# The last stage of a decoder step: residual rows read before the stage, and their sum moved from VectorE to Pool

## The chip, the cores and the metric

The kernel runs on one core of a Trainium2 chip. The metric is the device time of one execution in microseconds (us), the median of several. The engines are TensorE (PE, its weight loads PEld), VectorE (DVE), ScalarE (ACT), GpSimd (POOL, called Pool here) and SyncE (SP), which here only issues transfers. Each engine runs its own instructions in order; semaphores tie them together.

## The reference

One layer of a decoder step over 2048 prompt tokens and 32 sample tokens, 1024 channels. Two mixers and a mixture of experts (top 2 of 32) each add to the residual stream, and a last RMS norm follows. The part that matters here is the end:

```python
x = x + gate1 * (merged @ w_o)                 # x_after_mixers, kept in DRAM
...
y = routed_experts(h2, idx, wts, ...)          # two weighted rows for each token, summed
x = x + gate2 * y
...
y_prompt = x * rsqrt(mean(x * x) + EPS) * normf_g     # the same for y_sample
```

## The kernel before

The program has three blocks: `condition`, `sweep_mixers` and `finish`. The last part of `finish` is `experts`. Its main loop runs over blocks of 128 gathered rows, one expert to a block; each block ends with a scatter (L1913, an indirect transfer from Pool) of the weighted rows to `weighted_rows` in DRAM, two rows for each token. A transfer to `expert_gate_up` or `expert_down` brings an expert's weights into a ring of four slots.

After the last block comes the **last stage**, with which the change is concerned. It runs over 17 tiles: 16 of 128 tokens, and tile 16 with the 32 sample tokens. The work on tile i goes through all engines:

- SP reads the tile's pairs (`pairs`, L1792, 1 MB: two rows for each token) into one of NB = 4 buffers `pair`. Three lie in `expert_down`, the fourth in `gathered`.
- TensorE adds the two rows of each pair with 8 matmuls by the identity (L2204) into two banks of PSUM (named `fin` in the profile), and raises `paired`.
- VectorE multiplies by the gate row (L2109, two halves of 512 columns), raises `weighted`, adds the sum to the residual rows `xc(i)` (L2114), and raises `summed`.
- ScalarE squares the row and sums the squares (L2042, `sumsq`). Pool turns the sum into 1/rms with two small operations (L1941 `mean`, L1943 `root`), in the function `rms`. VectorE multiplies the row by it and by the norm's gain (L2118, the function `norm`, `done`), and ScalarE issues the store (L2047).

VectorE's order is `add(i)`, `norm(i - 1)`, so that the round over ScalarE and Pool for tile i - 1 has the time of `add(i)`. A pair buffer is free once `summed` is raised: then SP reads the pairs of tile i + 4.

The residual rows lie in the ring of the gate and up weights, which is free by then: `late_rows` gives NX = 8 places, in slots 0 and 2, and puts the three gate and gain rows into slot 1. Rows 0 to 7 are read before the stage, as soon as the slots are free (L1871). Rows 8 to 16 are read within the stage (L1895): the row of tile i + 8 takes the place of tile i, so SP waits until tile i's output is stored (`out_stored`). SP's own order puts this wait between the reads of pairs.

Of the kernel before, what the change touches and what calls it, by code (L numbers as in the profile page):

```python
# [7 lines left out]
F32 = mybir.dt.float32  # L8
# [3 lines left out]
ALU = mybir.AluOpType  # L12
# [129 lines left out]
def wait_apart(eng, sem, value, passed):  # L142

    eng.wait_ge(sem, value)
    eng.sem_inc(passed, 1)
# [1602 lines left out]
    return lists, ends_i, rest, on_vector, on_tensor  # L1748


def late_rows(ring):

    slot = lambda n: ring[:, n * GU:(n + 1) * GU].rearrange("p (k d) -> p k d", d=D)
    gates = [slot(1)[:, k, :] for k in range(3)]
    return (lambda at, m: slot(2 * (at % 8 // 4))[0:m, at % 4, :]), gates


def experts(nc, a, s, kept, sb, sem, ps, ring, downs, listing, ready, outs):
# [19 lines left out]
    down, y_out, stored = sem("e_down"), sem("e_y_out"), (sem("e_stored0"), sem("e_stored1"))  # L1778
    rec_in = [sem(f"e_rec_in{n}") for n in range(5)]
    x1_in, gates_in = sem("e_x1_in"), sem("e_gates_in")  # L1780
    NB, NX = 4, 8
    g_in, out_stored, late_in = [sem(f"c_pairs_in{k}") for k in range(NB)], [sem(f"c_stored{k}") for k in range(NX)], [sem(f"c_x1_in{k}") for k in range(NX)]
    paired, weighted, summed = sem("c_paired"), sem("c_weighted"), sem("c_summed")
    sumsq, mean, root, done = sem("c_sumsq"), sem("c_mean"), sem("c_root"), sem("c_done")
    xc, (gate, gate_s, gf) = late_rows(ring)
    sq = ring[:, GU + 3 * D:GU + 4 * D]
    pair = [downs[:, n * DOWN:(n + 1) * DOWN].rearrange("p (k d) -> p k d", k=2) for n in range(3)] + [xg[:, :, :]]
    t, minus_half = ready["rms"], kept["half"]
# [26 lines left out]
    def on_sync(sp):  # L1815
# [47 lines left out]
        for slot in (2, 3):  # L1863
            down_arrived(slot, NE // RING)

        x1, gates = late_rows(ring)
        for n, e in ((0, NE - 4), (1, NE - 2)):
            wait_apart(sp, w_lo, last_block(e) * 2, passed)
            for k in range(4):
# [2 lines left out]
            if n == 0:  # L1872
# [3 lines left out]
                             .to_broadcast([DEC_B, DEC_T, D])).then_inc(gates_in, 16)  # L1876
                sp.dma_start(gates[2], a["normf_g"].unsqueeze(0).to_broadcast([P, D])).then_inc(gates_in, 16)
        rest, total = listed(sp, REST, 0), listed(sp, TOTAL, 0)
        wait_apart(sp, stored[0], rest * 16 + 16, passed)
        wait_apart(sp, stored[1], total // 2 * 16, passed)  # L1880
        for n in range(3):
# [5 lines left out]
        for i in range(NT):  # L1887
            sp.wait_ge(summed, i + 1)
            if i + NB <= NT:
                pairs(sp, i + NB, P if i + NB < NT else MS)  # L1890
            late = i + NX - 2
            if i >= 2 and late <= NT:
                m = P if late < NT else MS
                sp.wait_ge(out_stored[(i - 2) % NX], 16 * ((i - 2) // NX + 1))
                sp.dma_start(x1(late, m), s["x1"][late * P:late * P + m, :]).then_inc(late_in[late % NX], 16)  # L1895

    def on_gpsimd(pool):
        pool.wait_ge(ready["lists"], 1)
        pool.wait_ge(ready["stored_x1"], 16 * (NT + 1))
        pool.wait_ge(ready["stored_h2"], 16 * (NT + 1))  # L1900

        def gather(b, slot, landed, first=False):

            if not first:
                wait_apart(pool, x_turned, b - 1, passed)
            wait_apart(pool, idx_in[slot], landed, passed)
            pool.indirect_dma_start(out=xg[:, slot % 2, :], out_offset=None, in_=s["h2"],  # L1907
                                    in_offset=bass.IndirectOffsetOnAxis(ap=idx[:, slot, 0:1].bitcast(U32), axis=0),
                                    bounds_check=TOKENS - 1, oob_is_err=False).then_inc(x_in[slot % 2], 16)

        def scatter(b, slot):
            wait_apart(pool, y_out, b + 1, passed)
            pool.indirect_dma_start(out=s["y2"], out_offset=bass.IndirectOffsetOnAxis(ap=rec[:, slot, 0:1].bitcast(U32), axis=0),  # L1913
                                    in_=y[:, half(slot), :], in_offset=None,
                                    bounds_check=2 * TOKENS - 1, oob_is_err=False).then_inc(stored[half(slot)], 16)

        def step(b, slot, landed):
            gather(b + 2, (slot + 2) % 4, landed)
            scatter(b - 1, (slot - 1) % 4)

        gather(0, 0, 16, True)
        gather(1, 1, 16, True)
        gather(2, 2, 16)
        total = listed(pool, TOTAL, 0)
        step(1, 1, 16)
        step(2, 2, 32)
        step(3, 3, 32)
        with pool.Fori(1, QUADS) as q:
            with pool.If(q * 4 < total):
                step(q * 4, 0, q * 16 + 16)  # L1930
                step(q * 4 + 1, 1, q * 16 + 16)
            with pool.If(q * 4 + 2 < total):
                step(q * 4 + 2, 2, q * 16 + 32)
                step(q * 4 + 3, 3, q * 16 + 32)
        rest = listed(pool, REST, 0)
        scatter(rest * 2 + 1, LAST)

        def rms(i, m):
            k = i % NB
            pool.wait_ge(sumsq, i + 1)  # L1940
            pool.tensor_scalar(t[0:m, k, 1:2], t[0:m, k, 0:1], 1.0 / D, EPS, ALU.mult, ALU.add).then_inc(mean, 1)  # L1941
            pool.wait_ge(mean, i + 1)
            pool.tensor_tensor(t[0:m, k, 2:3], t[0:m, k, 1:2], minus_half[0:m, :], ALU.pow).then_inc(root, 1)  # L1943

        for i, m in tiles():
            rms(i, m)
        wait_apart(pool, stored[0], rest * 16 + 16, passed)
        wait_apart(pool, stored[1], rest * 16 + 16, passed)

    def on_scalar(act):  # L1950
# [93 lines left out]
        def store(i, m):  # L2044
            dst = outs[0][0, i * P:(i + 1) * P, :] if i < NT else outs[1].rearrange("b t d -> (b t) d")
            act.wait_ge(done, i + 1)
            act.dma_start(dst, xc(i, m)).then_inc(out_stored[i % NX], 16)  # L2047

        for i, m in tiles():
            square(i, m)  # L2050
            if i:
                store(i - 1, P)
        store(NT, MS)
        for k in range(NX):
            act.wait_ge(out_stored[k], 16 * (NT // NX + (1 if k == 0 else 0)))
        for slot in range(4):
            wait_apart(act, idx_in[slot], (rest * 2 + (10 - slot)) // 4 * 16, passed)
            wait_apart(act, rec_in[slot], (rest * 2 + (6 - slot)) // 4 * 16, passed)
# [1 line left out]
    def on_vector(dve):  # L2060
# [40 lines left out]
                step(p * 2, 0)  # L2101
                step(p * 2 + 1, 1)

        def add(i, m):
            k, rows = i % NB, gate if i < NT else gate_s
            dve.wait_ge(paired, i + 1)
            for h in range(2):
                at = slice(h * 512, (h + 1) * 512)
                last = nc.vector.tensor_tensor(pair[k][0:m, 0, at], ps[2 * k + h][0:m, :], rows[0:m, at], ALU.mult)  # L2109
            last.then_inc(weighted, 1)  # L2110
            if i >= NX:
                dve.wait_ge(late_in[i % NX], i // NX * 16)
            dve.wait_ge(weighted, i + 1)
            nc.vector.tensor_tensor(xc(i, m), xc(i, m), pair[k][0:m, 0, :], ALU.add).then_inc(summed, 1)  # L2114

        def norm(i, m):
            dve.wait_ge(root, i + 1)
# [1 line left out]
                                           op0=ALU.mult, op1=ALU.mult).then_inc(done, 1)  # L2119

        dve.wait_ge(gates_in, 48)
        dve.wait_ge(x1_in, 16 * NX)
        for i, m in tiles():
            add(i, m)
            if i:
                norm(i - 1, P)
        norm(NT, MS)
# [86 lines left out]
def finish(nc, a, s, kept, outs):  # L2214

    with ExitStack() as ctx:
# [15 lines left out]
        with ExitStack() as gates:  # L2232
# [9 lines left out]
            g = gate_a(nc, a, s, kept, sem, ps, weights, shared)  # L2242
            b = gate_b(nc, a, s, kept, sem, ps, weights, shared, small, ready, early)
        late["ring"] = sb("expert_gate_up", [P, RING * GU])
        ready["split_weights"] = [[sb(f"gate_up{n}_{part}", [P, GU], F32R) for part in ("hi", "lo")] for n in range(2)]
        downs = sb("expert_down", [P, RING * DOWN])
        e = experts(nc, a, s, kept, sb, sem, ps, late["ring"], downs, listing, ready, outs)
# [57 lines left out]
```

## Time and profile before

| | us |
|---|---|
| median of 3 runs | 2117.55 |
| lowest and highest of the runs | 2117.15, 2119.03 |
| the profiled execution's own time | 2116.99 |
| its span, first to last instruction | 2114.6 |
| TensorE busy | 1954.3 |
| VectorE busy | 1090.1 |
| ScalarE busy | 752.9 |
| Pool busy | 329.8 |

The time of an execution is its span and what lies around it (2.4 us here). All places in the program are given in us from the start of the span. The last stage is the stretch from about 2020 us to the end. TensorE's busy share is that of the whole program, in which the stage is 1 part in 22; what bounds the stage has to be read from its own rows.

### The profile page before, as it was taken

The numbers are of one execution on the slowest core, as the hardware profiler recorded it, in microseconds if no ns is written. First come the engines' busy times: TensorE is split into PE (matmuls) and PEld (weight loads), VectorE is DVE, ScalarE is ACT, GpSimd is POOL, SyncE is SP. The second block draws the span as 40 slices with busy tenths as digits, with TensorE's granted clock in tenths as the row PEclk, the third lists the DMA queues.
The fourth block names the chain that finished last, engine by engine and source line by source line (L and its number), as shares of the span: only waits on it lengthen the run. The fifth ranks groups of instructions, "written<-read, shape, count | busy, mean of one in ns | idle before, by whom it ended". The sixth has DMA issues, their size and how long they took to land.

```text
span 2114.6 us, 29676 instructions
## 1 busy us (share of the span) xinstructions
PE 1954.3 (92%) x9239; PEld 1467.3 (69%) x9240; DVE 1090.1 (52%) x1905; ACT 752.9 (36%) x1318; POOL 329.8 (16%) x337
## 2 busy tenths in 40 slices
PE   6599999999869999999899999994699999999876
PEld 2487878778547777776788888873576777677532
DVE  2377777777440000003455555555566666666656
ACT  2245545444230101012321111111466666666611
POOL 0011100111000000000101111111143334333311
PEclk9799999999779999999999999996799999999988
DMA  9322222222185545544744444427487545889577
GB/s 297 105 92 92 102 102 100 102 84 94 30 290 198 193 160 189 206 159 165 270 143 149 146 145 149 143 70 261 150 301 272 213 163 176 296 284 363 202 286 282
DMA packets 193060, 381.87 MB, mean 181 GB/s; under 512 B 43113, under 2 KB 122137, under 8 KB 186828
## 3 DMA queue, kind: packets, MB, share of 16 engines
q1 hardware_dynamic: 153262, 313.07, 41.7%
q0 software_dynamic: 22000, 59.66, 7.4%
q10 hardware_dynamic: 17760, 8.67, 1.4%
q8 instruction: 20, 0.33, 0.1%
q14 instruction: 18, 0.15, 0.0%
HBM read 296.47 MB, written 104.26 MB: 189 GB/s over the span
## 4 chain that ended last, share of the span: by engine, by line
PE 62%; DMA 5%; DVE 2%; SPq 1%; issue 1%; ACT 0%; ACTq 0%; POOL 0%; DVEq 0%; POOLq 0%
PE fin L253 16%; PE fin L255 15%; PE fin L254 15%; PE fin L2169 8%; PE fin L2138 2%; PE fin L1605 1%; DMA expert_down<-weighted_rows 1%; PE fin L1632 1%; DMA w_gate_raw<-in_w_in 1%; DMA mixer_parts<-oT_split 1%; PE fin L2204 1%; PE fin L1184 1%; DMA slot_records<-slot_record,route_slots 1%; DMA pb_b<-out_b_projected 1%; PE fin L2157 0%
## 5 line engine op out<-in xcount | busy, mean ns | idle before, releaser
L2073 DVE TENSOR_TENSOR gate_up_lo<-expert_gate_up,gate_up_hi 128x2048 fp32r<-128x2048 f32 x102 | 233.6, 2292 | 147.4 <-ACT gate_up_hi L1977 143.4
L1977 ACT CAST gate_up_hi<-expert_gate_up 128x2048 fp32r x102 | 194.3, 1906 | 90.4 <-issue 90.4
L253 PE MATMUL mix<-w_mix_hi,hT_hi 128*128 128x512 f32 (+3 forms) x544 | 203.5, 374 | 3.9 <-DVE hT_lo L632 2.6
L254 PE MATMUL mix<-w_mix_hi,hT_lo 128*128 128x512 f32 (+3 forms) x544 | 198.9, 366 | 0.0
L255 PE MATMUL mix<-w_mix_lo,hT_hi 128*128 128x512 f32 (+3 forms) x544 | 198.5, 365 | 0.0
L1127 DVE SCALAR_TENSOR_TENSOR ma_rows<-tanh_rows,fin 128x512 f32<-128x512 f32 (+1 forms) x34 | 21.8, 683 | 339.1 <-PE fin L255 188.6
L2169 PE MATMUL fin<-expert_down,hidden_T 128*128 x400 | 183.0, 601 | 5.5 <-ACT hidden_T L1985 5.5
L253 PE MATMUL fin<-gate_up_hi,gathered_T_hi 128*128 128x512 f32 x400 | 162.0, 405 | 4.2 <-DVE gathered_T_lo L2064 4.2
L255 PE MATMUL fin<-gate_up_lo,gathered_T_hi 128*128 128x512 f32 x400 | 158.1, 395 | 0.0
L254 PE MATMUL fin<-gate_up_hi,gathered_T_lo 128*128 128x512 f32 x400 | 157.6, 394 | 0.0
L1907 POOL DMA_INDIRECT gathered<-h_rows,row_tokens x52 | 130.9, 2517 | 42.4 <-issue 23.9
L2169 PEld LDWEIGHTS fin<-expert_down,hidden_T 128*128 128x128 f32 x400 | 73.2, 193 | 79.4 <-issue 79.3
L253 PEld LDWEIGHTS mix<-w_mix_hi,hT_hi 128*128 128x128 f32 (+1 forms) x544 | 100.6, 185 | 37.2 <-issue 20.3
L253 PE MATMUL fin<-w_gate_hi,h_parts 128*128 128x512 f32 (+1 forms) x272 | 110.8, 407 | 14.2 <-DMA h_parts<-hT_split 12.1
L255 PEld LDWEIGHTS mix<-w_mix_lo,hT_hi 128*128 128x128 f32 (+1 forms) x544 | 100.5, 185 | 19.2
L254 PEld LDWEIGHTS mix<-w_mix_hi,hT_lo 128*128 128x128 f32 (+1 forms) x544 | 100.8, 185 | 16.4
L1913 POOL DMA_INDIRECT weighted_rows<-y_block,row_records x50 | 62.5, 1250 | 305.8 <-ACT y_block L1993 293.9
L253 PE MATMUL fin<-w_out_hi,merged_T_hi 128*128 128x512 f32 (+1 forms) x272 | 107.8, 396 | 1.1 <-ACT merged_T_hi L1387 1.1
L254 PE MATMUL fin<-w_gate_hi,h_parts 128*128 128x512 f32 (+1 forms) x272 | 108.7, 400 | 0.0
L255 PE MATMUL fin<-w_gate_lo,h_parts 128*128 128x512 f32 (+1 forms) x272 | 108.3, 398 | 0.0
L253 PE MATMUL fin<-w_gate_hi,h_parts_b 128*128 128x512 f32 (+1 forms) x272 | 107.9, 397 | 0.0
L253 PE MATMUL fin<-w_out_hi,mixer_parts 128*128 128x512 f32 (+1 forms) x272 | 106.3, 391 | 1.4 <-DVE w_out_lo L1113 1.3
(302 smaller groups left out, 3865.1 us busy)
## 6 DMA issues: line engine op xcount, KB each, us to landing
expert_gate_up<-in_w_gate SPq DMA_DIRECT2D x32, 1024.0 KB
expert_gate_up<-in_w_up SPq DMA_DIRECT2D x32, 1024.0 KB
expert_down<-in_w_down SPq DMA_DIRECT2D x32, 1024.0 KB
h_parts<-hT_split SPq DMA_DIRECT2D x16, 1024.0 KB, 5.1
mixer_parts<-oT_split SPq DMA_DIRECT2D x32, 512.0 KB, 8.3
w_ada_part<-in_w_ada SPq DMA_DIRECT2D x16, 1024.0 KB, 10.6
h_parts_b<-hT_split SPq DMA_DIRECT2D x16, 1024.0 KB, 4.8
expert_down<-weighted_rows SPq DMA_DIRECT2D x12, 1024.0 KB, 9.7
```

The costliest lines, as they stand in the source:

```text
L253: nc_mm(out, left[0], right[0], start=first, stop=False)
L254: nc_mm(out, left[1], right[0], start=False, stop=False)
L255: return nc_mm(out, left[0], right[1], start=False, stop=last)
L1127: last = nc.vector.scalar_tensor_tensor(out=ma[0:m, par, at], in0=tg[0:m, at], scalar=1.0, in1=ps[2 + n][0:m, :], op0=ALU.add, op1=ALU.mult)
L1184: done = nc.tensor.matmul(ps[6 + half][32 * j:32 * j + R, :], c_now[half][:, :], wc[half][:, j, :], start=first, stop=last, tile_position= ...
L1605: last = nc.tensor.transpose(ps[bank + k // 4][:, (k % 4) * P:(k % 4) * P + m], src[0:m, k * P:(k + 1) * P], ident[0:m, 0:m])
L1907: pool.indirect_dma_start(out=xg[:, slot % 2, :], out_offset=None, in_=s["h2"], in_offset=bass.IndirectOffsetOnAxis(ap=idx[:, slot, 0:1].b ...
L1913: pool.indirect_dma_start(out=s["y2"], out_offset=bass.IndirectOffsetOnAxis(ap=rec[:, slot, 0:1].bitcast(U32), axis=0), in_=y[:, half(slot ...
L1977: nc.scalar.copy(wg[par][0][:, n * HG:(n + 1) * HG], ring[:, bass.ds(slot * GU + n * HG, HG)]).then_inc(w_hi, 1)
L2073: nc.vector.tensor_tensor(wg[par][1][:, at], ring[:, bass.ds(slot * GU + n * HG, HG)], wg[par][0][:, at].bitcast(F32), ALU.subtract).then_ ...
L2138: last = nc.tensor.transpose(ps[k // 4][:, (k % 4) * P:(k % 4 + 1) * P], xg[:, par, k * P:(k + 1) * P], ident[:, :])
L2169: last = nc.tensor.matmul(ps[5 + n][:, :], hT[par][:, k, :], downs[:, bass.ds(at, 512)], start=(k == 0), stop=(k == 1))
```

## The change

Two things change, both in the last stage.

First, `late_rows` gives a place to each of the 17 residual tiles: eight as before, four in slot 3 of the ring, and five in `late_x1`, a new tile that lies where the split gate and up weights (`gate_up_hi` and `gate_up_lo`) were. SP issues the nine reads of tiles 8 to 16 before it reads the first pairs; it waits for the last split of weights (`w_lo`) and the last gate and up matmul (`gu`), which were the last users of these places. The waits for `out_stored` within the stage are gone, and its eight semaphores are one.

Second, the sum with the residual rows is an instruction of Pool, in the same form (128 x 1024, float32), ahead of `rms(i - 1)`. VectorE keeps the multiplication by the gate, now called `weigh`, and `norm`.

```diff
-def late_rows(ring):
+def late_rows(ring, spare):
     slot = lambda n: ring[:, n * GU:(n + 1) * GU].rearrange("p (k d) -> p k d", d=D)
     gates = [slot(1)[:, k, :] for k in range(3)]
-    return (lambda at, m: slot(2 * (at % 8 // 4))[0:m, at % 4, :]), gates
+    rows = [slot(n)[:, k, :] for n in (0, 2, 3) for k in range(4)] + [spare[:, k, :] for k in range(NT + 1 - 12)]
+    return (lambda at, m: rows[at][0:m, :]), gates
...
-    NB, NX = 4, 8
+    NB, NX, NS = 4, 8, 12
...
         rest, total = listed(sp, REST, 0), listed(sp, TOTAL, 0)
+        wait_apart(sp, w_lo, rest * 4 + 8, passed)
+        wait_apart(sp, gu, rest * 2 + 2, passed)
+        for at in range(NX, NT + 1):
+            m = P if at < NT else MS
+            sp.dma_start(x1(at, m), s["x1"][at * P:at * P + m, :]).then_inc(late_in[at // NS], 16)
         wait_apart(sp, stored[0], rest * 16 + 16, passed)
...
             sp.wait_ge(summed, i + 1)
             if i + NB <= NT:
                 pairs(sp, i + NB, P if i + NB < NT else MS)
-            late = i + NX - 2
-            if i >= 2 and late <= NT:
-                m = P if late < NT else MS
-                sp.wait_ge(out_stored[(i - 2) % NX], 16 * ((i - 2) // NX + 1))
-                sp.dma_start(x1(late, m), s["x1"][late * P:late * P + m, :]).then_inc(late_in[late % NX], 16)
...
+        def add(i, m):
+            k = i % NB
+            if i == NX:
+                pool.wait_ge(late_in[0], 16 * (NS - NX))
+            if i == NS:
+                pool.wait_ge(late_in[1], 16 * (NT + 1 - NS))
+            pool.wait_ge(weighted, i + 1)
+            pool.tensor_tensor(xc(i, m), xc(i, m), pair[k][0:m, 0, :], ALU.add).then_inc(summed, 1)
+
+        pool.wait_ge(x1_in, 16 * NX)
         for i, m in tiles():
-            rms(i, m)
+            add(i, m)
+            if i:
+                rms(i - 1, P)
+        rms(NT, MS)
...
-        def add(i, m):
+        def weigh(i, m):
             k, rows = i % NB, gate if i < NT else gate_s
             dve.wait_ge(paired, i + 1)
             for h in range(2):
                 at = slice(h * 512, (h + 1) * 512)
                 last = nc.vector.tensor_tensor(pair[k][0:m, 0, at], ps[2 * k + h][0:m, :], rows[0:m, at], ALU.mult)
             last.then_inc(weighted, 1)
-            if i >= NX:
-                dve.wait_ge(late_in[i % NX], i // NX * 16)
-            dve.wait_ge(weighted, i + 1)
-            nc.vector.tensor_tensor(xc(i, m), xc(i, m), pair[k][0:m, 0, :], ALU.add).then_inc(summed, 1)
...
         for i, m in tiles():
-            add(i, m)
+            weigh(i, m)
             if i:
                 norm(i - 1, P)
         norm(NT, MS)
```

The change moves instructions on three engines. Pool before, from the last scatter to its third `rms` (`c_sumsq` is the sum of squares from ScalarE):

```order
L1913 DMA weighted_rows<-y_block,row_records 4160x1024 [waits e_y_out]
L1941 TENSOR_SCALAR rms_c<-rms_c 128x1 [waits c_sumsq]
L1943 TENSOR_TENSOR rms_c<-rms_c,minus_half_row 128x1 [waits c_mean]
L1941 TENSOR_SCALAR rms_c<-rms_c 128x1 [waits c_sumsq]
L1943 TENSOR_TENSOR rms_c<-rms_c,minus_half_row 128x1 [waits c_mean]
L1941 TENSOR_SCALAR rms_c<-rms_c 128x1 [waits c_sumsq]
L1943 TENSOR_TENSOR rms_c<-rms_c,minus_half_row 128x1 [waits c_mean]
```

Pool now, from the same scatter (`c_weighted` comes from VectorE, after the multiplication by the gate):

```order
L1914 DMA weighted_rows<-y_block,row_records 4160x1024 [waits e_y_out]
L1953 TENSOR_TENSOR expert_gate_up<-expert_gate_up,expert_down 128x1024 [waits c_weighted,e_x1_in]
L1953 TENSOR_TENSOR expert_gate_up<-expert_gate_up,expert_down 128x1024 [waits c_weighted]
L1942 TENSOR_SCALAR rms_c<-rms_c 128x1 [waits c_sumsq]
L1944 TENSOR_TENSOR rms_c<-rms_c,minus_half_row 128x1 [waits c_mean]
L1953 TENSOR_TENSOR expert_gate_up<-expert_gate_up,expert_down 128x1024 [waits c_weighted]
L1942 TENSOR_SCALAR rms_c<-rms_c 128x1 [waits c_sumsq]
L1944 TENSOR_TENSOR rms_c<-rms_c,minus_half_row 128x1 [waits c_mean]
```

The sums stand between the small operations: tile i's sum, with its wait for VectorE, comes ahead of the two operations of tile i - 1.

VectorE before, in the middle of the stage, tiles 8 and 9, each followed by the norm of the tile before (`c_paired` comes from TensorE, `c_root` from Pool):

```order
L2109 TENSOR_TENSOR expert_down<-fin,expert_gate_up 128x512 [waits c_paired]
L2109 TENSOR_TENSOR expert_down<-fin,expert_gate_up 128x512
L2114 TENSOR_TENSOR expert_gate_up<-expert_gate_up,expert_down 128x1024 [waits c_weighted,c_x1_in0]
L2118 SCALAR_TENSOR_TENSOR expert_gate_up<-expert_gate_up,rms_c 128x1024 [waits c_root]
L2109 TENSOR_TENSOR expert_down<-fin,expert_gate_up 128x512 [waits c_paired]
L2109 TENSOR_TENSOR expert_down<-fin,expert_gate_up 128x512
L2114 TENSOR_TENSOR expert_gate_up<-expert_gate_up,expert_down 128x1024 [waits c_weighted,c_x1_in1]
L2118 SCALAR_TENSOR_TENSOR expert_gate_up<-expert_gate_up,rms_c 128x1024 [waits c_root]
```

VectorE now, the same two tiles:

```order
L2122 TENSOR_TENSOR expert_down<-fin,expert_gate_up 128x512 [waits c_paired]
L2122 TENSOR_TENSOR expert_down<-fin,expert_gate_up 128x512
L2127 SCALAR_TENSOR_TENSOR expert_gate_up<-expert_gate_up,rms_c 128x1024 [waits c_root]
L2122 TENSOR_TENSOR expert_down<-fin,expert_gate_up 128x512 [waits c_paired]
L2122 TENSOR_TENSOR expert_down<-fin,expert_gate_up 128x512
L2127 SCALAR_TENSOR_TENSOR expert_gate_up<-expert_gate_up,rms_c 128x1024 [waits c_root]
```

The sum is gone from between the multiplication and the norm; the order of what stays, and its waits, are the same.

SP before, from its first wait for the last scatters (`e_stored`) on:

```order
L144 ISA
L144 ISA [waits e_stored0]
L1792 DMA expert_down<-weighted_rows 128x2048 [waits e_stored1]
L1792 DMA expert_down<-weighted_rows 128x2048 x2
L144 REGISTER_ALU
L144 ISA [waits e_x_in0,e_x_in1]
L1792 DMA gathered<-weighted_rows 128x2048 [waits e_x_turned]
L1792 DMA expert_down<-weighted_rows 128x2048 [waits c_summed] x3
L1895 DMA expert_gate_up<-x_after_mixers 128x1024 [waits c_stored0]
L1792 DMA gathered<-weighted_rows 128x2048 [waits c_summed]
```

SP now, from the same place (`late_x` is `late_x1`, printed without its number):

```order
L144 ISA
L144 ISA [waits e_w_lo]
L1884 DMA expert_gate_up<-x_after_mixers 128x1024 [waits e_gate_up]
L1884 DMA expert_gate_up<-x_after_mixers 128x1024 x3
L1884 DMA late_x<-x_after_mixers 128x1024 x4
L1884 DMA late_x<-x_after_mixers 32x1024
L144 ISA
L144 ISA [waits e_stored0]
L1793 DMA expert_down<-weighted_rows 128x2048 [waits e_stored1]
L1793 DMA expert_down<-weighted_rows 128x2048 x2
L144 REGISTER_ALU
L144 REGISTER_ALU [waits e_x_in0,e_x_in1]
```

The nine reads of residual rows stand ahead of the wait for the last scatters, and no read of pairs has a wait for a store ahead of it.

## Rows read from the trace of the kernel before

**Rows 1.** The page: the span of the profiled execution.

```profile
span 2114.6 us, 29676 instructions
```

**Rows 2.** Stretches: us, each engine's busy us, PEclk, DMA share, GB/s.

```profile
2033.40:2051.00 17.60, 17.16 (x40) 7.24 (x39) 17.39 (x20) 5.34 (x11) 3.70 (x10) 1.00 0.96 356
2051.00:2072.00 21.00, 16.50 (x32) 6.32 (x32) 15.54 (x17) 5.44 (x10) 3.65 (x10) 0.92 1.02 422
2072.00:2092.40 20.40, 16.27 (x33) 6.72 (x34) 14.75 (x16) 4.60 (x8) 2.99 (x9) 0.92 1.02 403
```

**Rows 3.** Transfers from 2015 us: name, count, KB each, us to landing.

```profile
expert_down<-weighted_rows SPq DMA_DIRECT2D x12, 1024.0 KB, 9.7
...
expert_gate_up<-x_after_mixers SPq DMA_DIRECT2D x8, 512.0 KB, 10.3
```

**Rows 4.** SP's waits from 2000 us: total us, times, longest.

```profile
SPq L1895 <- DMA out<-expert_gate_up: 26.3, 9, 4.9
```

**Rows 5.** Waits of the last stage, the same columns.

```profile
DVE expert_down L2109 <- PE fin L2204: 33.8, 6, 23.1
PE fin L2204 <- DMA expert_down<-weighted_rows: 17.3, 6, 9.9
```

**Rows 6.** Timeline of one tile: start us, us, engine, line, operation.

```profile
2046.86 1.28 DVE L2118 SCALAR_TENSOR_TENSOR expert_gate_up<-expert_gate_up,rms_c 128x1024 f32<-128x1024 f32 x1
...
2047.04 1.06 ACT L2042 ACTIVATE expert_gate_up<-expert_gate_up 128x1024 f32<-128x1024 f32 x1 [2.50 <-DVE expert_gate_up L2114]
...
2048.05 1.28 DVE L2109 TENSOR_TENSOR expert_down<-fin,expert_gate_up 128x512 f32<-128x512 f32 x2
...
2048.27 0.19 POOL L1941 TENSOR_SCALAR rms_c<-rms_c 128x1 f32<-128x1 f32 x1 [2.83 <-ACT expert_gate_up L2042]
2048.55 0.55 POOL L1943 TENSOR_TENSOR rms_c<-rms_c,minus_half_row 128x1 f32<-128x1 f32 x1
...
2049.37 1.23 DVE L2114 TENSOR_TENSOR expert_gate_up<-expert_gate_up,expert_down 128x1024 f32<-128x1024 f32 x1
```

**Rows 7.** Timeline of the last tile, VectorE and Pool.

```profile
2099.86 1.27 DVE L2109 TENSOR_TENSOR expert_down<-fin,expert_gate_up 32x512 f32<-32x512 f32 x2
2101.23 1.21 DVE L2114 TENSOR_TENSOR expert_gate_up<-expert_gate_up,expert_down 32x1024 f32<-32x1024 f32 x1
...
2104.04 0.54 POOL L1943 TENSOR_TENSOR rms_c<-rms_c,minus_half_row 32x1 f32<-32x1 f32 x1
...
2104.61 1.27 DVE L2118 SCALAR_TENSOR_TENSOR expert_gate_up<-expert_gate_up,rms_c 32x1024 f32<-32x1024 f32 x1 [0.97 <-POOL rms_c L1943]
```

**Rows 8.** Timeline, where the pipeline fills.

```profile
2024.84 11.99 PE L2204 MATMUL fin<-expert_down,identity 128*128 128x512 f32 x24 [9.90 <-DMA expert_down<-weighted_rows]
...
2033.43 1.29 DVE L2109 TENSOR_TENSOR expert_down<-fin,expert_gate_up 128x512 f32<-128x512 f32 x2 [0.79 <-PE fin L2204]
```

**Rows 9.** Pool's groups by shape: count | busy us, mean ns.

```profile
L478 POOL TENSOR_SCALAR_AFFINE_SELECT w_s_rows<-w_s_rows 128x512 f32<-128x512 f32 x1 | 0.6, 640 | 0.0
...
L453 POOL MEMSET minus_half<- 128x1 f32 x1 | 0.1, 98 | 13.1 <-POOLq L131 13.1
```

**Rows 10.** Timeline at 228 us, VectorE and Pool.

```profile
227.60 2.29 DVE L729 TENSOR_TENSOR scores<-scores,tiny 128x2048 f32<-128x2048 f32 x1
...
228.38 1.56 POOL L462 TENSOR_SCALAR tiny<-tiny 128x1 f32<-128x1 f32 x1 [21.56 <-ACT squares L495]
```

**Rows 11.** The hand-over: timeline, and one stretch.

```profile
2004.71 2.29 DVE L2073 TENSOR_TENSOR gate_up_lo<-expert_gate_up,gate_up_hi 128x2048 fp32r<-128x2048 f32 x1 [0.66 <-ACT gate_up_hi L1977]
...
2009.00:2017.00 8.00, 5.94 (x8) 2.02 (x6) 0.00 (x0) 1.26 (x2) 0.00 (x0) 0.68 0.00 0
...
2017.27 0.99 POOL L1913 DMA_INDIRECT weighted_rows<-y_block,row_records  x1 [12.34 <-ACT y_block L1993]
2019.94 1.28 SPq L1792 DMA_DIRECT2D expert_down<-weighted_rows  x3
```

**Rows 12.** Timeline, TensorE after a pause.

```profile
2057.94 5.40 PE L2204 MATMUL fin<-expert_down,identity 128*128 128x512 f32 x8 [2.46 <-DMA expert_down<-weighted_rows]
```

## What the change will do to the time

> **What bounds the kernel now.** The page comes first: its span, 2114.6 us, is what the sum below is made against [rows 1]. The execution itself took 2116.99 us, 0.56 us under the median of 2117.55. TensorE's share of the whole program says nothing of the last stage, so I read that stage from its stretches next. They show two phases. Up to 2051 us VectorE is busy in 17.39 of 17.60 us and is the bound. Its three groups follow one another: norm to multiplication takes 1.19 us, multiplication to sum 1.32, and the sum is 1.23 us long, about 3.7 us for a tile [rows 6]. From 2051 to 2092 us VectorE is busy in 30.3 of 41.4 us, while the 16 transfer engines are busy all the time and move 403 to 422 GB/s [rows 2]. So transfers bound that phase: a tile moves 1.05 MB of pairs, 0.52 MB of residual rows and 0.52 MB of output, 2.10 MB, which at 413 GB/s is 5.1 us. The views of transfers and waits agree: a read of pairs lands 9.7 us after issue and a read of residual rows after 10.3 [rows 3]; TensorE waits for pairs and VectorE for TensorE, though both totals hold the first wait of the stage, 9.9 and 23.1 us [rows 5]; and SP stands 26.3 us in waits for a store before it may read residual rows, with reads of pairs queued behind [rows 4]. Over both phases multiplication 1 starts at 2033.43 and multiplication 16 at 2099.86 [rows 7, 8], so a tile takes 66.43 / 15 = 4.43 us. That is the number to compare with.
>
> **Part 1: residual rows in advance.** Nine reads, 4.3 MB, go out when the last split of weights is done, at 2004.71 + 2.29 = 2007.0 us; the last gate and up matmul, the other wait, is earlier, because that split already belongs to a block that is never multiplied. From 2009 to 2017 us nothing moves [rows 11]. At 413 GB/s the nine reads need 10.5 us. With about 2 us from issue to flow (pairs issued at 2019.94 let TensorE begin at 2024.84 [rows 8, 11]) they flow from about 2009 to 2019.5. The last scatter is issued at 2017.27 and had landed by 2019.94, when the pairs go out [rows 11]. It now shares the engines with the last 2 us of the reads. That delays the first pairs by nothing at best and by 3 us at worst (if the reads run at 356 GB/s, the least of [rows 2], they end at 2021.2 and the scatter and pairs queue behind what is left). I take 0.7 us, nearer the low end, because the two meet for 2 us at most and the scatter (0.5 MB) needs only a part of the engines. The DMA issues on SP take no time that matters: before, SP waited there for the scatter.
>
> Within the stage a tile then moves 1.57 MB, 3.8 us at 413 GB/s, and SP's 26.3 us of waits for stores are gone. By itself this part would take the second phase from 5.1 us a tile to 3.8, a gain of some 10 us over its 8 tiles. Whether it is seen depends on part 2.
>
> **Part 2: the sum on Pool.** VectorE loses 1.23 us a tile. But the order of instructions closes a circle. VectorE does the multiplication of tile i, then the norm of tile i - 1. That norm waits for Pool's root of tile i - 1, and on Pool the root now stands behind the sum of tile i, which waits for the multiplication of tile i. Nothing of a tile can run beside the next: multiplication i, sum i, mean and root i - 1, norm i - 1, multiplication i + 1 are one chain. The period is its length:
>
> - norm to next multiplication, start to start: 2048.05 - 2046.86 = 1.19 us [rows 6];
> - multiplication, 1.28 us [rows 6], and the hop to Pool. The nearest hop is VectorE's to ScalarE or ScalarE's to Pool, some 0.1 us: the sum of the last tile ends at 2102.44 and the last norm starts 2.17 us later, with a square of 1.06 us and its read-out, mean and root in between [rows 6, 7]. Together 1.38 us;
> - the sum on Pool, S, below;
> - Pool's next instruction, 0.08 us later (2048.27 + 0.19 to 2048.55 is 0.09), then mean and root: 2048.27 to 2049.10 is 0.83 us [rows 6]. The sum of squares of tile i - 1 has long been there: ScalarE began it when sum i - 1 ended;
> - root to norm: 2104.04 + 0.54 to 2104.61 is 0.03 us [rows 7].
>
> So the period is 3.51 us + S. No row shows a Pool operation on two inputs of this size. The nearest is one on a single input, 128x512 in 640 ns; with 98 ns for an operation on one element, it costs 1.06 ns an element [rows 9]. If two inputs of 1024 stream side by side, S = 1.18 us, the low bound. If two reads and the write take turns, S = 3.35 us, the high bound. If the two reads take turns and the write runs beside them, S = 2.27 us. I take this one, since the single-input row already holds a read and a write side by side, and only the second read is new. The Trainium skill, "GPSIMD Engine Reference", section 3.1, has a measured price: a float32 `tensor_tensor` add of 2048 elements takes 4497 ns, which is an estimate of 2.25 us for 1024. By that page the sum would be 0.3 us less; no run here shows it yet.
>
> The period is 3.51 + 2.27 = 5.78 us against 4.43 now.
>
> **The sum.** Multiplication 1 starts as before, when TensorE has tile 1 (2033.43), since the first tiles still wait for pairs and TensorE. Multiplication 16 then starts 15 x 5.78 = 86.7 us later, at 2120.13. From there to the last norm: 1.38 us, S = 2.27, and 2.17 us over ScalarE and Pool, which is 2125.95 against 2104.61 now [rows 7]. That is 21.3 us more, and with 0.7 us of later start 22.0 us. What follows the last norm (its end, a small store, the end of the program) stays. On the profiled execution's own time: 2116.99 + 22.0 = 2139.0 us; with the 0.56 us to the median, 2139.6, which I round to 2139.5 us, 1.04% slower.
>
> What hides the rest: at 5.78 us a tile the transfers need 3.8, VectorE 2.5 and TensorE 3.4 us, and a pair buffer, read again when its sum ends, has 4 x 5.78 less 1.38 and 2.27, 19.5 us, until its next multiplication. So the gain of part 1 lies wholly beside the chain.
>
> **The rivals.**
>
> *TensorE becomes the bound.* With pauses of over 2 us in each tile its clock may drop. After a pause of 2.46 us eight matmuls took 5.40 us [rows 12], and the stretches with pauses show a granted clock of 0.92 [rows 2]. At full clock (1.00, 2.4 GHz) 40 matmuls took 17.16 us [rows 2], 3.43 us a tile; at the lower level (0.50, 1.2 GHz) it would be twice that, 6.86. If the clock stayed there, the period would be 6.86, 16.2 us more over 15 tiles, less the 7.6 us by which TensorE can be late (19.5 us from a sum's end to the next multiplication from that buffer, less 4.9 for the read [rows 8, 11] and 6.86): 2148 us. Against it: at 6.86 us a tile TensorE would not pause at all, and in the stretch in which it hardly pauses the clock is 1.00 [rows 2].
>
> *The order does not bind, and the sum is hidden* (the other side). If the root of tile i - 1 came ahead of sum i, as ScalarE's timing would allow, transfers would set 3.8 us. One thing speaks against even this gain: a Pool operation on one element began at 228.38 and ended at 229.94, 1.56 us in place of 0.19 for the same form [rows 6], just after a VectorE operation with two inputs in SBUF had ended (229.89) [rows 10]. Norm and sum exclude each other, then: 2.27 + 0.9 + 1.2 is 4.4 us a tile, no change, 2117.5 us. The Trainium skill, "SBUF — State Buffer", section "SBUF: two separate sides", tells of this as an exclusive lock on a port pair that VectorE and GpSimd share; the trace agrees with its 1.56 us. It costs nothing in my forecast, where norm and sum never meet. This rival decides only if Pool's instructions ran in another order than written. The same result would come from a cheap sum: the chain is at 4.43 us for S = 0.92, below the low bound. At S = 1.18 it would be 2122.
>
> *The sum is dearer or cheaper than two turns.* Each 0.1 us of S is 16 x 0.1 = 1.6 us. S = 1.65 gives 2129.6, S = 2.9 gives 2149.7, S = 3.35 gives 2156.9.
>
> **Chances.** My forecast, the chain with S from 1.65 to 2.9: 0.80. A dearer sum: 0.07. A cheaper one, 1.18 to 1.65 (2122 to 2130): 0.06. TensorE at the lower clock: 0.04. No change, the sum hidden: 0.03, of which 0.01 is faster. The range is the forecast's own, 2130 to 2150, which also holds the start's 0 to 3 us and TensorE's case. A measurement of this kernel can tell about 0.2%, 4.2 us, from no change; so faster 0.01, same 0.03, slower 0.96.
>
> **What would show it.** Right: on Pool, sum, mean and root follow one another with one wait each tile, for VectorE's multiplication; VectorE's norm waits each time for Pool's root, some 3.3 us; multiplications start 5.8 us apart from tile 1 on; the transfers' share falls from 1.02 to some 0.65; nine residual reads between 2007 and 2011 us, and pairs issued by 2021 us. Wrong: S far from 2.3 us; VectorE waiting for TensorE in the middle of the stage; norms that start before the sum of the next tile is done; pairs landing late, or the first multiplication more than 2 us late.

## The result: 1.1% slower, with one tile's chain as long as forecast

The changed kernel took 2140.89 us (median of 4 runs, 2139.01 to 2143.06) against 2118.0 us for the kernel before, run beside it (4 runs, 2117.15 to 2119.03). The ratio is 1.0108, with a 95% interval from 1.0091 to 1.0126. Forecast were 2139.5 us in a range from 2130 to 2150. The profiled execution took 2141.08 us.

The page of the changed kernel:

```profile
span 2138.4 us, 29670 instructions
...
PE 1952.7 (91%) x9239; PEld 1466.4 (69%) x9240; DVE 1070.3 (50%) x1888; ACT 753.1 (35%) x1318; POOL 370.9 (17%) x354
```

The span grew from 2114.6 [rows 1] to 2138.4 us, while TensorE's busy time is what it was. The stage's stretches (columns as in [rows 2]):

```profile
2009.00:2017.00 8.00, 3.85 (x6) 1.35 (x4) 0.00 (x0) 1.26 (x2) 0.99 (x1) 0.71 1.01 402
...
2033.40:2060.00 26.60, 21.65 (x50) 8.88 (x48) 11.22 (x14) 5.74 (x10) 14.60 (x14) 1.00 0.75 266
2060.00:2090.00 30.00, 21.98 (x41) 8.64 (x42) 12.41 (x15) 5.75 (x10) 16.11 (x16) 0.89 0.76 269
2090.00:2115.00 25.00, 14.45 (x32) 4.85 (x31) 10.16 (x13) 5.68 (x10) 13.45 (x15) 0.92 0.50 181
```

Before, VectorE filled the first phase and the transfer engines the second [rows 2]. Now neither does: VectorE is busy 41% of the time, the transfers' share is 0.50 to 0.76, and TensorE pauses too. When all engines idle in part of every tile, something may go in a circle. The chain of waits shows it, here for one tile (start, us, what; "issue" is a hop between engines):

```profile
2045.76 1.21 DVE gathered L2122 x2
2046.97 0.07 issue
2047.04 2.34 POOL expert_gate_up L1953
2049.38 0.08 issue
2049.46 0.20 POOL rms_c L1942
2049.66 0.07 issue
2049.74 0.56 POOL rms_c L1944
2050.30 0.03 issue
2050.32 1.28 DVE expert_gate_up L2127
2051.61 1.21 DVE expert_down L2122 x2
```

From one multiplication (L2122) to the next: its result at 2046.97, sum on Pool (L1953) 2.34 us, mean (L1942), root (L1944), norm on VectorE (L2127), and the next multiplication. From 2045.76 to 2051.61 is 5.85 us, in which VectorE and Pool never work at once. The view of waits says the same from the other side (total us, times, longest), to be held against [rows 5]:

```profile
DVE expert_gate_up L2127 <- POOL rms_c L1944: 40.5, 12, 3.4
POOL expert_gate_up L1953 <- DVE expert_down L2122: 35.1, 9, 15.9
DVE expert_down L2122 <- PE fin L2212: 27.8, 2, 25.7
```

VectorE waits 3.4 us in each tile for Pool's root, which before it waited for once, 1.0 us long, at the very end [rows 7]. Pool waits 2.6 us in each tile, from the third on, for VectorE's multiplication. VectorE's waits for TensorE are two, both where the pipeline fills: behind the fill TensorE is not the bound. The groups give the mean of the new instruction (busy us, mean ns):

```profile
L1953 POOL TENSOR_TENSOR expert_gate_up<-expert_gate_up,expert_down 128x1024 f32<-128x1024 f32 x9 | 21.1, 2342 | 35.1 <-DVE expert_down L2122 35.1
...
L2127 DVE SCALAR_TENSOR_TENSOR expert_gate_up<-expert_gate_up,rms_c 128x1024 f32<-128x1024 f32 x12 | 15.4, 1284 | 40.5 <-POOL rms_c L1944 40.5
```

The sum takes 2.34 us on Pool, against 1.23 on VectorE [rows 6]. The norm is as fast as before, 1.28 us. A read of pairs now lands in 5.1 us, where it was 9.7 [rows 3]:

```profile
expert_down<-weighted_rows SPq DMA_DIRECT2D x12, 1024.0 KB, 5.1
```

So the reads in advance did free the transfer engines. But nothing waited for the freed time. The hand-over to the stage, with TensorE's and VectorE's first work:

```profile
2005.15 1.76 SPq L1884 DMA_DIRECT2D expert_gate_up<-x_after_mixers  x4
2006.95 2.99 SPq L1884 DMA_DIRECT2D late_x<-x_after_mixers  x5
...
2015.18 0.99 POOL L1914 DMA_INDIRECT weighted_rows<-y_block,row_records  x1 [12.36 <-ACT y_block L2007]
...
2019.63 1.29 SPq L1793 DMA_DIRECT2D expert_down<-weighted_rows  x3
...
2024.55 12.79 PE L2212 MATMUL fin<-expert_down,identity 128*128 128x512 f32 x24 [11.70 <-DMA expert_down<-weighted_rows]
...
2033.95 1.29 DVE L2122 TENSOR_TENSOR expert_down<-fin,expert_gate_up 128x512 f32<-128x512 f32 x2 [2.08 <-PE fin L2212]
```

The nine reads go out at 2005.15 and 2006.95, the scatter at 2015.18, and the pairs, which wait for its data, at 2019.63: 4.45 us later, where it was 2.67 [rows 11]. TensorE begins at 2024.55, and multiplication 1 at 2033.95, 0.5 us later than before [rows 8].

The last tile, VectorE (DVE) and Pool in turn:

```profile
2121.82 1.27 DVE L2122 TENSOR_TENSOR expert_down<-fin,expert_gate_up 32x512 f32<-32x512 f32 x2
...
2123.17 2.33 POOL L1953 TENSOR_TENSOR late_x<-late_x,expert_down 32x1024 f32<-32x1024 f32 x1 [2.59 <-DVE expert_down L2122]
...
2126.44 1.28 DVE L2127 SCALAR_TENSOR_TENSOR late_x<-late_x,rms_c,expert_gate_up 128x1024 f32<-128x1024 f32 x1 [3.36 <-POOL rms_c L1944]
...
2126.82 0.95 POOL L1942 TENSOR_SCALAR rms_c<-rms_c 32x1 f32<-32x1 f32 x1 [0.41 <-ACT expert_gate_up L2056]
...
2128.43 1.27 DVE L2127 SCALAR_TENSOR_TENSOR late_x<-late_x,rms_c,expert_gate_up 32x1024 f32<-32x1024 f32 x1 [0.70 <-POOL rms_c L1944]
```

Multiplication 16 starts at 2121.82, the sum on Pool 1.35 us later, and the last norm at 2128.43. In between, the mean of 32 partitions (L1942) takes 0.95 us in place of 0.19: it began while the norm of tile 15, 2126.44 to 2127.72, was running.

### The profile page after: what moved, and what is told of

Its sections match the earlier page's. It is cut to its first block, busy times and chain, and to the rows that moved or that the text cites. A ratio compares the mean times of both kernels' runs of the same rounds, so it can differ in the third digit from the quotient of the medians.

```text
span 2138.4 us, 29670 instructions
## 1 busy us (share of the span) xinstructions
PE 1952.7 (91%) x9239; PEld 1466.4 (69%) x9240; DVE 1070.3 (50%) x1888; ACT 753.1 (35%) x1318; POOL 370.9 (17%) x354
## 4 chain that ended last, share of the span: by engine, by line
PE 61%; DMA 4%; DVE 3%; POOL 2%; issue 1%; SPq 1%; ACT 0%; ACTq 0%; DVEq 0%; POOLq 0%
PE fin L253 15%; PE fin L254 15%; PE fin L255 15%; PE fin L2177 8%; PE fin L2146 2%; PE fin L1605 1%; POOL expert_gate_up L1953 1%; PE fin L1632 1%; DMA w_gate_raw<-in_w_in 1%; DMA mixer_parts<-oT_split 1%; DVE expert_gate_up L2127 1%; PE fin L1184 1%; DVE expert_down L2122 1%; POOL late_x L1953 1%; DMA pb_b<-out_b_projected 1%
```

## The experiments

Two theories stood against each other at first. **The chain**: Pool's order (sum of tile i ahead of the root of tile i - 1) ties each tile to the next, and the length of that chain is the period. **The price**: Pool is slow or gets in VectorE's way, and the order has no part in it. A third question was what the reads in advance cost and give by themselves. All times below are medians, and ratios are to the kernel before on the same chip.

### Each half of the change by itself

`rows_only` keeps the reads in advance and gives the sum back to VectorE:

```diff
-            pool.tensor_tensor(xc(i, m), xc(i, m), pair[k][0:m, 0, :], ALU.add).then_inc(summed, 1)
...
             last.then_inc(weighted, 1)
+            dve.wait_ge(weighted, i + 1)
+            nc.vector.tensor_tensor(xc(i, m), xc(i, m), pair[k][0:m, 0, :], ALU.add).then_inc(summed, 1)
```

> Part 1 alone: the nine residual reads in advance, the sum stays on VectorE. Theory (the loss is the chain that Pool's order closes): no chain, so VectorE and TensorE set 3.66 to 3.8 us a tile in place of 4.43. With a start 2.6 us later (the last scatter took 4.4 us beside the reads, in place of 2.6), that is 2117.5 + 2.6 - 15 x 0.7 = 2109 to 2111 us. Rival (reads in advance cost more than they give, by crowding the hand-over): 2118 us or more.

Measured: 2107.2 us (2105.8 to 2110.2), ratio 0.9953 (0.9937 to 0.997). The whole stage in one stretch, and the second and the last multiplication:

```profile
2035.40:2090.00 54.60, 53.57 (x120) 20.92 (x118) 53.94 (x60) 17.14 (x31) 11.14 (x30) 1.00 0.93 370
...
2035.35 1.29 DVE L2109 TENSOR_TENSOR expert_down<-fin,expert_gate_up 128x512 f32<-128x512 f32 x2 [0.79 <-PE fin L2206]
...
2090.32 1.27 DVE L2109 TENSOR_TENSOR expert_down<-fin,expert_gate_up 32x512 f32<-32x512 f32 x2
```

VectorE is busy 53.94 of 54.60 us, TensorE 53.57. A tile takes (2090.32 - 2035.35) / 15 = 3.66 us to the end of the stage, where before the period rose to 5.1 us in the second phase. The reads in advance are a gain of 11 us by themselves, about 1 us more than the prediction gave them, and the change shows none of it. They gave more than the 2109 to 2111 us expected of this run: multiplication 1 came 1.9 us later than before the change, not 2.6, and the period is at the low end of the 3.66 to 3.8 us. Little was left here for a faster VectorE, too: TensorE needs 3.43 us a tile even without a pause [rows 2], 0.23 us less than VectorE's 3.66, so a sum moved away at no cost could have won at most some 3.5 us over 15 tiles (an estimate from these two figures).

`sum_only` is the kernel before with the sum on Pool; residual rows are read within the stage as they were:

```diff
+            pool.wait_ge(weighted, i + 1)
+            pool.tensor_tensor(xc(i, m), xc(i, m), pair[k][0:m, 0, :], ALU.add).then_inc(summed, 1)
...
-            nc.vector.tensor_tensor(xc(i, m), xc(i, m), pair[k][0:m, 0, :], ALU.add).then_inc(summed, 1)
```

> Part 2 alone: the sum on Pool, residual rows still read within the stage. Theory: the chain is 5.85 us a tile whoever reads the rows when (2.10 MB in 5.85 us is 359 GB/s, under the 413 reached). 15 x (5.85 - 4.43) = 21.3 us, and 1.2 us at the last tile: 2140 us. Rival (part of the changed kernel's loss is the reads in advance): 2136 us or less. Rival (the transfers bind as well once residual reads are back): over 2145 us.

Measured: 2140.22 us (2139.5 to 2141.69), ratio 1.0107 (1.009 to 1.0124). That is the changed kernel's time. A tile takes (2121.78 - 2033.55) / 15 = 5.88 us:

```profile
2033.55 1.29 DVE L2120 TENSOR_TENSOR expert_down<-fin,expert_gate_up 128x512 f32<-128x512 f32 x2 [2.08 <-PE fin L2210]
...
2121.78 1.27 DVE L2120 TENSOR_TENSOR expert_down<-fin,expert_gate_up 32x512 f32<-32x512 f32 x2
```

The sum on Pool costs 22 us where the rows are read within the stage. Where they are read in advance it costs 34 us (2107.2 against 2140.89), because it also hides all that the reads in advance give.

### The order, and what stands behind it

`root_first` turns the two on Pool:

```diff
         for i, m in tiles():
-            add(i, m)
             if i:
                 rms(i - 1, P)
+            add(i, m)
         rms(NT, MS)
```

> The changed kernel with Pool's order turned: mean and root of tile i - 1 ahead of the sum of tile i. Theory (the order makes the chain): Pool waits for ScalarE's square instead, the round is sum 2.34, square and hops 1.4, mean and root 0.83, that is 4.65 us a tile if norm and sum may run together: 2123 us. If they exclude each other, the norm, released at the same moment as the sum, waits for the sum: 2.34 + 1.19 + 1.38 = 4.9 us, 2127 us; if the sum waits for the norm, 5.9 us, no gain, 2141 us. Rival (the order does not matter, Pool's price alone does): 2141 us.

Measured: 2132.43 us (2131.4 to 2133.93), ratio 1.007 (1.0053 to 1.0087). The order does matter, 8.5 us of it, with the same instructions. But 2132 lies between two of the cases, and the timeline shows why. Sometimes the sum starts first and sometimes the norm, in turn (start us, duration us, engine, line; L1953 is the sum, L2127 the norm, L2122 the multiplication):

```profile
2048.71 2.34 POOL L1953 TENSOR_TENSOR expert_gate_up<-expert_gate_up,gathered 128x1024 f32<-128x1024 f32 x1
2048.78 3.36 DVE L2127 SCALAR_TENSOR_TENSOR expert_gate_up<-expert_gate_up,rms_c 128x1024 f32<-128x1024 f32 x1 [3.19 <-POOL rms_c L1944]
...
2052.06 1.27 DVE L2122 TENSOR_TENSOR expert_down<-fin,expert_gate_up 128x512 f32<-128x512 f32 x2
...
2053.26 1.27 DVE L2127 SCALAR_TENSOR_TENSOR expert_gate_up<-expert_gate_up,rms_c 128x1024 f32<-128x1024 f32 x1
2053.42 3.32 POOL L1953 TENSOR_TENSOR expert_gate_up<-expert_gate_up,expert_down 128x1024 f32<-128x1024 f32 x1 [0.21 <-DVE expert_down L2122]
2054.45 1.27 DVE L2122 TENSOR_TENSOR expert_down<-fin,expert_gate_up 128x512 f32<-128x512 f32 x2
...
2058.85 2.35 POOL L1953 TENSOR_TENSOR expert_gate_up<-expert_gate_up,expert_down 128x1024 f32<-128x1024 f32 x1
```

At 2048.71 the sum starts, and 0.07 us later the norm. The norm takes 3.36 us in place of 1.28: it ends at 2052.14, 1.09 us after the sum's end at 2051.05. In the next tile the norm comes first, at 2053.26, and now the sum takes 3.32 us in place of 2.34: the norm is in its way until 2054.53. From sum to sum it is 4.71 us where the norm waits (4.9 were expected) and 5.43 us where the sum waits (5.9 were expected), 5.1 us a tile in the mean. So the sum on Pool and the norm on VectorE exclude each other: whichever comes second waits, and its recorded duration holds the wait. [rows 10] had shown it for one small operation.

`two_behind` takes all waits between neighbours away, to see whether that exclusion alone would be left (ScalarE's stores move to tile i - 2 in the same way):

```diff
-            add(i, m)
-            if i:
-                rms(i - 1, P)
+            if i >= 2:
+                rms(i - 2, P)
+            add(i, m)
...
             weigh(i, m)
-            if i:
-                norm(i - 1, P)
+            if i >= 2:
+                norm(i - 2, P)
```

> The changed kernel with no chain: Pool makes mean and root of tile i - 2 ahead of the sum of tile i, VectorE the norm of tile i - 2 behind the multiplication of tile i, ScalarE stores tile i - 2. Nothing of a tile waits for its neighbour. Theory (norm, with two inputs in SBUF, and Pool's work exclude each other): sum 2.34, mean and root 0.83 with gaps, norm 1.2 in turn, 4.4 to 4.6 us a tile: 2119 to 2122 us, no faster than before the change. Rival (they only met by chance, and run side by side): transfers set 3.75 us, 2109 us.

Measured: 2120.86 us (10 runs, 2116.0 to 2124.12), ratio 1.0011 (0.9999 to 1.0022). As forecast by the exclusion, and 12 us from the rival. In the timeline sum, norm and Pool's mean follow in one file:

```profile
2063.22 2.34 POOL L1953 TENSOR_TENSOR expert_gate_up<-expert_gate_up,gathered 128x1024 f32<-128x1024 f32 x1
...
2063.29 3.35 DVE L2129 SCALAR_TENSOR_TENSOR expert_gate_up<-expert_gate_up,rms_c 128x1024 f32<-128x1024 f32 x1 [1.96 <-POOL rms_c L1944]
...
2065.65 1.05 POOL L1942 TENSOR_SCALAR rms_c<-rms_c 128x1 f32<-128x1 f32 x1
```

The norm, started 0.07 us behind the sum, ends at 2066.64. The mean on Pool, an operation on one element that takes 0.19 us elsewhere, starts at 2065.65 and ends at 2066.70, just behind the norm. The multiplication (one input in SBUF, the other in PSUM) is not held up: the one at 2054.45 in `root_first` takes its usual 1.27 us while a sum is under way. The period is 4.39 us, from 2036.36 to 2102.18 over 15 tiles. The exclusion is thus what stands behind the order. That 4.39 is close to the 4.43 us of the kernel before says little, since there transfers bound the second phase. The kernel that differs only in where the sum runs and in the order is `rows_only`, with 3.66 us a tile and 2107 us: beside it, the sum on Pool loses 14 us even with the chain undone.

### The price of the sum

`half_sum` is the changed kernel with the sum over 512 columns in place of 1024; the other half of each row gets no residual addition.

```diff
-            pool.tensor_tensor(xc(i, m), xc(i, m), pair[k][0:m, 0, :], ALU.add).then_inc(summed, 1)
+            pool.tensor_tensor(xc(i, m)[:, 0:512], xc(i, m)[:, 0:512], pair[k][0:m, 0, 0:512], ALU.add).then_inc(summed, 1)
```

> The changed kernel, in which Pool adds only the first 512 of the 1024 columns (the other half of each row is left without its residual addition). If the chain of which the sum is one link sets the period, it falls by all that the sum gets shorter: the sum 1.2 us, the period 3.51 + 1.2 = 4.7 us, 2140.9 - 16 x 1.15 = 2122.5 us. If something else sets it (reads of pairs, TensorE's clock), the period stays above 5 us. It also gives the price of an element: 2.34 us for 1024 and what 512 take.

Measured: 2124.32 us, a single execution, so without an interval; 2122.5 was expected. Two sums in a row on Pool:

```profile
2045.63 1.26 POOL L1953 TENSOR_TENSOR expert_gate_up<-expert_gate_up,gathered 128x512 f32<-128x512 f32 x1 [2.60 <-DVE gathered L2122]
...
2050.40 1.26 POOL L1953 TENSOR_TENSOR expert_gate_up<-expert_gate_up,expert_down 128x512 f32<-128x512 f32 x1 [2.60 <-DVE expert_down L2122]
```

1.26 us for 512 columns, 4.77 us from one to the next, which is 3.51 + 1.26. So the whole of the sum is in the period, and the rest of the chain is the 3.51 us of the prediction. From 512 to 1024 columns the sum grows by 1.08 us, 2.11 ns for a column, twice the 1.06 ns that [rows 9] gives for one input. That fits the case of two reads in turns.

### What the reads in advance cost

`reads_after_pairs` is the changed kernel with the nine reads of residual rows moved behind the first four reads of pairs (the two waits and the loop, as they stand, after `pairs(sp, 3, P)`).

> The changed kernel with the nine residual reads issued behind the first four reads of pairs. Theory: the reads in advance delayed the last scatter and the first pairs by 2.6 us; that goes, the period stays at 5.85 us: 2138.3 us. Rival (the late start has another cause, such as TensorE's clock): 2141 us. If the chain did not bind, the residual reads in the stage would show as a longer period.

Measured: 2137.54 us (2136.04 to 2138.76), ratio 1.0092 (1.0075 to 1.0109), 3.3 us under the changed kernel, whose own ratio of 1.0108 lies within this interval. The last scatter, and the first reads of pairs, which wait for it:

```profile
2013.91 0.98 POOL L1914 DMA_INDIRECT weighted_rows<-y_block,row_records  x1 [12.25 <-ACT y_block L2007]
...
2016.57 1.28 SPq L1793 DMA_DIRECT2D expert_down<-weighted_rows  x3
```

2.66 us apart, as before the change (2.67, [rows 11]), where the changed kernel has 4.45. The reads in advance did delay the scatter.

The time does not show that gain by itself. The period did not stay at 5.85 us as expected: it is (2119.66 - 2030.03) / 15 = 5.98 us, because one tile took 7.67 us while TensorE waited 6.32 us for pairs that were issued behind the nine reads. That gives the 1.8 us back. What is left of the 3.3 us comes from elsewhere: the profiled execution reached its last scatter 1.3 us earlier, its first 24 matmuls took 11.98 us in place of 12.79, and 1.6 us of it lie outside the span in place of 2.7.

`rows_split` leaves the sum on VectorE and sends four of the nine reads ahead, five behind the first pairs:

```diff
-        for at in range(NX, NT + 1):
+        for at in range(NX, NS):
...
         pairs(sp, 3, P)
+        for at in range(NS, NT + 1):
+            m = P if at < NT else MS
+            sp.dma_start(x1(at, m), s["x1"][at * P:at * P + m, :]).then_inc(late_in[1], 16)
```

> Part 1 alone, but only four of the nine residual reads go out ahead of the last scatter (2.1 MB, 5 us, landed some 3 us before the scatter is issued), the other five behind the first four reads of pairs. Theory (the last scatter took 1.5 to 2.1 us longer beside the reads): it takes 2.7 us again and pairs go out 2 us earlier: 2105.2 us. Rival (the five reads crowd the reads of pairs, since 1.57 MB in 3.66 us is already 429 GB/s): 2107 us or more.

It ran with `rows_only` once more:

> Part 1 alone once more, as the measure for the next two kernels on the same chip. It ran in 2107.2 us before; every theory expects 2107 us, within 2.

Measured: `rows_only_again` 2107.24 us (2105.28 to 2108.97), ratio 0.995 (0.9937 to 0.9963); `rows_split` 2105.08 us (6 runs, 2102.88 to 2112.39), ratio 0.9947 (0.9931 to 0.9962). The reads, the scatter and the pairs in `rows_split`:

```profile
2003.85 1.76 SPq L1884 DMA_DIRECT2D expert_gate_up<-x_after_mixers  x4
...
2013.71 0.98 POOL L1917 DMA_INDIRECT weighted_rows<-y_block,row_records  x1 [12.19 <-ACT y_block L1997]
...
2016.37 1.27 SPq L1793 DMA_DIRECT2D expert_down<-weighted_rows  x3
...
2018.45 2.45 SPq L1895 DMA_DIRECT2D late_x<-x_after_mixers  x5
```

The scatter's data are there 2.66 us after its issue again, against 4.78 in `rows_only` and 4.27 in `rows_only_again`. The medians differ by 2.2 us, near the 1.6 to 2.1 that this should give, but the two intervals overlap nearly wholly, so a gain in time is not shown. `rows_split` has the lowest median of all. It beats the kernel before by 0.5%, as `rows_only` does.

## Why the prediction was right

**What bounds the stage.** Two phases, VectorE and then transfers: confirmed by `rows_only`, in which the second phase runs at the first one's pace, 3.66 us, once residual reads and waits for stores are out of it. It takes out both at once, so no run shows how much of the 5.1 us was bandwidth and how much the waits. The forecast gain of part 1 by itself, some 10 us, was 11.2 us.

**The chain.** Read from the order of instructions, it is there link by link, and its part without the sum measured 5.85 - 2.34 = 3.51 us, the prediction's figure. From multiplication 1 to 16 the changed kernel takes 2121.82 - 2033.95 = 87.87 us against 66.43: 5.86 us a tile where 5.78 was forecast, and 21.4 us more than before, of the 24.1 by which the two profiled executions differ. That the chain is the cause is shown by three experiments that keep the instructions and change their order or length: `root_first`, `two_behind` and `half_sum`.

**The price of the sum.** S was taken as 2.27 us, two reads in turns, and is 2.34, 3% more: 1.1 us in all. `half_sum` gives 2.11 ns a column, twice the price of one input, which fits the two turns; no run shows what makes the price so. The page "GPSIMD Engine Reference" of the Trainium skill, section 3.1, gave 2.25 us by halving its measured 2048 elements; the trace has 4% more than that estimate.

**The start.** This term was mis-sized. The prediction gave 0.7 us for the nine reads beside the last scatter; the scatter took 4.45 us to the next read in place of 2.67, so 1.8 us. The reads lasted to about 2017 at 402 GB/s and met the scatter, issued at 2015.18, for some 2 us, as reckoned. But they cost nearly all of these 2 us and not a third. A further 0.8 us came from TensorE, whose first 24 matmuls took 12.79 us in place of 11.99 [rows 8]. The granted clock shows where it went, in the first 6 us of these matmuls before and after (columns as in [rows 2]):

```profile
2024.84:2030.84 6.00, 6.00 (x11) 2.78 (x12) 0.74 (x2) 0.00 (x0) 0.00 (x0) 0.76 1.00 425
...
2024.55:2030.55 6.00, 6.00 (x9) 2.64 (x10) 0.00 (x0) 0.00 (x0) 0.00 (x0) 0.62 1.03 434
```

TensorE had paused for 9.9 and 11.7 us, and both times it begins at a clock of 0.50, the lower level; now it stays there longer, so the mean is 0.62 against 0.76. In the other runs the 24 matmuls took from 11.98 to 13.61 us, and 13.33 in `sum_only`, which has no reads in advance, so no run ties this to the change. In the profiled execution most of the two together, 2.6 us, is cancelled: it reached the last scatter 2.1 us earlier than that of before (2015.18 against 2017.27). The code ahead of it is the same in both, and over all kernels here this place varies from 2013.7 to 2017.5 us.

**The last tile.** From multiplication 16 to the last norm 6.61 us, against 4.75 before and 5.82 forecast. The sum is 0.07 of the 0.8 us over the forecast. The rest is the mean of tile 16, 0.95 us in place of 0.19: it ended at 2127.77, just behind the norm of tile 15. The prediction said that exclusion costs nothing because norm and sum never meet. They never do; but this norm and this mean do.

The terms add up: -2.1 (before the stage) + 2.6 (start) + 21.4 (15 periods) + 1.9 (last tile) + 0.3 (outside the span, 2.7 against 2.4) = 24.1 us. The forecast was 22.0. It was low by 1.2 us for the 15 periods, 0.8 for the last tile, 1.9 for the start and the 0.3 outside the span, 4.2 us in all, and the 2.1 us before the stage, of which it had nothing, took half of that back. That is luck. Between the medians the difference is 22.9 us, within 1 us of the forecast. The mechanism and the length of the chain were right; a match that close is partly luck.

**The rivals.** TensorE did pause between most tiles, by up to 2.6 us, and one group of eight matmuls took 5.26 us, but VectorE never waited for it after the fill. (In that rival's sum the 7.6 us should be 7.7, which changes nothing.) The rival on the other side, the sum hidden, was said to end at no change because norm and sum exclude each other. With the order that it named, `root_first`, a tile took 5.1 us, so for that order it was too low: sum and norm still met in every tile, and in every second one it was the sum that waited. With one more tile between sum and root, `two_behind`, it took 4.39 us, the 4.4 us of the prediction, and that kernel ran in 2120.86 us against 2117.5 forecast for the rival. The Trainium skill, "SBUF — State Buffer", section "SBUF: two separate sides", has the rule that such a pair is locked for a whole instruction and that the loser blocks fully; the trace agrees, with 3.36 us for a norm of 1.28 behind a sum of 2.34. By a rule of shared bandwidth both would have been slower at once, which no row shows: the first of the two always took its usual time.

## What to carry to other kernels

Before moving an operation to an idle engine, write down what stands ahead of what on both engines, and follow the waits around. If the new operation comes ahead of something that the giving engine waits for, the two engines make one chain, and the gain in busy time is worth nothing. Then ask whether the two engines can run at once at all: here a sum on Pool and a norm on VectorE, each with two inputs in SBUF, could not, and the period grew from 3.66 to 4.39 us even with the chain undone. Look also at what the third engine leaves to be won: TensorE needed 3.43 us a tile. And test the halves of a change apart; here one half gained 11 us by itself, and the other lost 22 by itself and hid the 11 as well.

## What the runs showed of the hardware that was not expected

The exclusion works both ways, and is written into the durations: 3.36 us for a norm of 1.28, 3.32 us for a sum of 2.34, 1.05 and 0.95 us for a mean of 0.19. A duration above its group's usual can therefore be a wait, to be looked for on the other engine. A sum over 32 partitions takes as long as one over 128 (2.33 and 2.34 us). And a burst of reads delays a scatter that is issued near its end by nearly the whole rest of the burst: 2.66 or 2.67 us from issue to use in the four profiled executions without reads in flight at that point, 4.15 to 5.07 us in the six with them.
